# A recurrent layer's scans and roots in another order, an output product begun early, and the small products of the first projection moved

## The chip, the cores and the metric

The kernel runs on one core of a Trainium2 chip. It is one launch that computes the whole reference. The metric is the device time of the launch in microseconds (us), median over runs. The kernel is written engine by engine: each engine (TensorE, VectorE, ScalarE, GpSimd and the queue of SyncE) has a list of instructions of its own, and they meet only through semaphores. The order of each engine's list is the order of the code.

## The reference

Everything is float32. 512 tokens of 1024 channels go through two blocks:

```python
def first_block(...):            # one layer
    mod = silu(c) @ w_ada + b_ada                  # 6 vectors of 1024
    h = rmsnorm(x) * (1 + scale1) + shift1
    y = mixer(h)   # h @ w_in, causal convolution, gated delta rule and windowed attention, @ w_out
    x = x + gate1 * y
    h = rmsnorm(x) * (1 + scale2) + shift2
    x = x + gate2 * moe(h)       # 32 experts, top 4
def second_block(...):           # two layers; the modulation of each: silu(c_2) @ ada_w_2 + ada_b_2
    # layer 0: windowed attention, then mlp;  layer 1: recurrent_block, then mlp
def recurrent_block(h):
    z = h @ w_in;  xr, gate = split(z, 2)          # 1536 channels each
    xr = conv4(xr)                                  # centred depthwise convolution over 4 tokens
    for each direction (forward, reverse):
        r = sigmoid(xr @ w_a + b_a);  i = sigmoid(xr @ w_x + b_x)    # 16 blocks of 96 channels
        log_a = -8 * r * softplus(-lam);  a = exp(log_a)
        u = sqrt(-expm1(2 * log_a)) * (i * xr)
        h_t = a_t * h_(t-1) + u_t                   # scan over the tokens
    return ((h_forward + h_reverse) * gelu(gate)) @ w_out
```

In the mixer the decays need two small groups of columns of the first projection, `h @ w_in[:, 2048:2056]` (four channels a, four channels b).

## The kernel before

**The projection of the mixer** (`proj_pe`, `proj_act`, `proj_dve`). TensorE makes four column groups of 512: i = 0 to 2 are q, k and v (channels on partitions, convolved by VectorE), i = 3 is the gate z (tokens on partitions, four tiles t of 128 tokens), i = 4 the attention's queries, i = 5 its keys and values. The eight columns a and b are made in between, in two steps: line 518 makes four partial sums in one bank, ScalarE copies them to `abpart` (line 615, behind its twelve SiLUs of the convolutions), and four small products (line 544) with the selector `absel` add and turn them. These stand in the middle of the first tile of i = 3: at (i, t, k) = (3, 0, 4). `abw`, `absel` and `abpart` lie in rows 0 and 1 of `mixed`, which the SiLU of z overwrites tile by tile (line 621). VectorE then makes a, b ready (lines 578 to 583).

**The side sums.** At the same time VectorE multiplies 40 half slices of the modulation matrices (1 MB each) by the vector silu(c) and adds them up (`side_dve`, lines 376 and 378; called "half sums" here). They come through one slot of two halves: SyncE loads a half again when VectorE has read it (lines 165 and 333). After each eight of them TensorE sums over the partitions (`side_pe`, lines 397 and 385), ScalarE copies the result (`ada_act`, line 417) and sends it to DRAM with four DMAs (line 422). Sums 3 and 4 come last. VectorE's order is: half sums up to the 27th, then a wait for the sums of squares of TensorE (lines 586 and 588, released by line 526), the 28th, the decays' steps (lines 591 to 597), and the last twelve. All four compute engines then meet (`meet`, line 192), and the delta rule begins (line 712).

**The recurrent layer** (`rnn_pe`, `rnn_act`, `rnn_dve`, `rnn_pool`). Its input projection runs in eight steps of three channel tiles, in the order x0 x1 x2 z0 x3 z1 z2 z3 (line 2757). The gates run in eight units k = 2b + d (b a group of three channel tiles, d the direction): `gates(k, m)` is line 2771. In step i TensorE's order is gates(k, 0), gates(k, 1), block(i, 0), gates(k, 2), block(i, 1), for step 4 also all gates of unit 4, and block(i, 2). The gates have two pairs of banks, so gates(k, m) waits until ScalarE has read the gates two before (`gate_read`).

For each unit ScalarE does `front(k)`: two sigmoids for each tile (lines 2827, 2828), three tanh (2834), three exp (2838); and later `roots(k)`: one sqrt over three tiles (2842). Between different functions it loads a table. GpSimd squares the decays (2881). VectorE does `gate_in(k)` (2922, waits for all sigmoids), `one_minus(k)` (2928, waits for the squares; the sqrt waits for it), `scans(k)` (2935 waits for the sqrt, 2939 or 2941 are three scans, 2944 adds the two directions), and the convolutions `conv(n)` (2909 to 2917), each of which frees its bank for the next block of TensorE. `gelus` (2850) and `gated` (2951) make the last factor.

**The output product** (`rnn3_pe`, line 3001). Two halves h of 512 columns, for each of four token tiles t, sum over twelve channel tiles n. The weights lie in four slots, `RO_SLOT[h][n // 6]`: 2 and 4 for h = 0, 3 and 5 for h = 1. The order for t = 0 is slot 2, 4, 3, 5. It starts when all twelve tiles are gated. `rnn_out_sp` loads slot 2 early, slot 3 after unit 6, and slots 4 and 5 after the last scan; behind them stand the weights of the next layer. GpSimd's two loads of the layer norm start when all is gated. With t = 0, h = 0 finished, VectorE begins the residual (line 2044).

The order of the work around the change is written out by hand in `rnn_act` and `rnn_dve`; no planner is involved.

## Time and profile before

| | us |
|---|---|
| median of 3 runs | 3044.62 (3043.0 to 3049.29) |
| the profiled execution, its own time | 3045.79 |
| its span in the trace | 3044.1 |
| TensorE busy (matmuls) | 2788.8, 92% of the span |
| VectorE busy | 1134.7, 37% |
| ScalarE busy | 465.7, 15% |
| GpSimd busy | 235.7, 8% |

The projection of the mixer lies at 59 to 232 us of the span, the experts fill the middle, and the recurrent layer lies at 2290 to 2620 us. Positions in the text are us from the start of the span. "Granted clock" is TensorE's clock in a stretch as a share of full speed; 1.00 is 2.4 GHz and 0.50 is 1.2 GHz. Each matmul of float32 shows as two MATMUL instructions, so 8 products are "x16".

### The profile page before, as it was taken

Reading aid. Unit: us, or ns where it says so; the run is one execution under the profiler, and the core shown is the slowest. Engines: PE = TensorE matmul, PEld = TensorE weight load, DVE = VectorE, ACT = ScalarE, POOL = GpSimd, SP = SyncE. Lnnn points to the kernel's source line nnn. Section 1 sums busy time; section 2 is a strip of 40 time slices with the busy share of each in tenths; the row PEclk is TensorE's granted clock in tenths of the full one; section 3 lists DMA queues with packets and bytes.
Section 4 is the critical chain, followed back from the end, with each engine's and each line's share of the span. In section 5 each row is a group of like instructions: output and inputs, shape, how many; then the busy total and the mean of one; then the engine's idle time right before and its main releaser. Section 6 shows DMA issues by size and latency. Waiting matters only on the chain.

```text
span 3044.1 us, 37477 instructions
## 1 busy us (share of the span) xinstructions
PE 2788.8 (92%) x15695; PEld 1377.0 (45%) x15695; DVE 1134.7 (37%) x1419; ACT 465.7 (15%) x916; POOL 235.7 (8%) x364
## 2 busy tenths in 40 slices
PE   7898989698999999998996999999999988999998
PEld 3355765232323333333332465467654333546763
DVE  3855453411111111211114153455436552344544
ACT  1112042010000000000001143000023552200001
POOL 1000011111110011011011500000000100000000
PEclk9998989799999999999997999999999999999999
DMA  9765411889999999999998122122123223221310
GB/s 332 281 244 218 184 29 47 327 326 399 394 389 402 395 403 406 398 406 397 412 396 335 9 103 70 48 91 99 66 60 75 51 62 110 104 81 58 110 56 28
DMA packets 211795, 639.50 MB, mean 210 GB/s; under 512 B 75908, under 2 KB 77532, under 8 KB 170898
## 3 DMA queue, kind: packets, MB, share of 16 engines
q1 hardware_dynamic: 197778, 607.76, 52.9%
q0 software_dynamic: 13792, 29.39, 3.4%
q8 instruction: 120, 1.97, 0.3%
q14 instruction: 41, 0.33, 0.0%
q10 hardware_dynamic: 64, 0.07, 0.0%
HBM read 626.44 MB, written 15.23 MB: 211 GB/s over the span
## 4 chain that ended last, share of the span: by engine, by line
PE 51%; issue 33%; DVE 4%; DMA 4%; POOL 3%; POOLq 2%; ACT 2%; DVEq 1%; SPq 0%; ACTq 0%
PE ps L2421 10%; PE ps L2456 10%; PE ps L2757 4%; PE ps L2492 4%; PE ps L2136 3%; PE ps L3001 3%; PE ps L2388 2%; PE ps L2407 2%; PE ps L2303 2%; DMA slots<-in_ada_w_dram 2%; PE ps L1213 2%; POOLq L1656 2%; DMA slots<-in_w_ada_dram 2%; POOL work L1665 1%; PE ps L2771 1%
## 5 line engine op out<-in xcount | busy, mean ns | idle before, releaser
L1767 PE MATMUL ps<-slots,hT 128*32 128x512 f32 x5120 | 579.1, 598 | 17.5 <-DMA slots<-in_w_up_dram 6.7
L1767 PEld LDWEIGHTS ps<-slots,hT 128*32 128x32 f32 x5120 | 159.0, 110 | 412.8 <-issue 399.4
L2456 PE MATMUL ps<-slots,work 128*128 128x512 f32 x672 | 290.0, 593 | 5.3 <-DVE work L2532 2.8
L1803 PE MATMUL ps<-slots,work 128*32 128x512 f32 x2112 | 254.5, 609 | 26.6 <-DMA slots<-in_w_down_dram 19.3
L1918 DVE TENSOR_SCALAR stage<-ps 128x512 f32<-128x512 f32 (+1 forms) x47 | 32.2, 686 | 580.9 <-PE ps L1769 580.5
L2456 PEld LDWEIGHTS ps<-slots,work 128*128 128x128 f32 x672 | 127.2, 190 | 166.4 <-issue 162.0
L2421 PE MATMUL ps<-hT,slots 128*128 128x256 f32 x768 | 169.2, 380 | 4.7 <-issue 4.7
L1803 PEld LDWEIGHTS ps<-slots,work 128*32 128x32 f32 x2112 | 89.8, 111 | 157.2 <-issue 125.0
L2421 PEld LDWEIGHTS ps<-hT,slots 128*128 128x128 f32 x768 | 145.4, 190 | 29.1 <-issue 9.5
L2757 PE MATMUL ps<-hT,slots 128*128 128x512 f32 x352 | 156.8, 601 | 0.5
L2629 DVE TENSOR_TENSOR work<-work,ps 128x1024 f32<-128x1024 f32 x60 | 71.6, 1218 | 168.8 <-PE ps L2456 168.5
L1896 ACT ACTIVATE modA<-stage 128x512 f32<-128x512 f32 (+1 forms) x47 | 29.6, 630 | 635.9 <-DVE stage L1918 635.9
L2492 PE MATMUL ps<-slots,work 128*128 128x512 f32 x256 | 114.3, 608 | 5.3 <-DVE work L2594 5.3
L1938 DVE COPY modB<-ps 128x512 f32<-128x512 f32 x33 | 22.8, 691 | 229.6 <-PE ps L1806 221.9
L2757 PEld LDWEIGHTS ps<-hT,slots 128*128 128x128 f32 x352 | 66.3, 192 | 92.5 <-issue 92.5
L2588 DVE TENSOR_TENSOR work<-work,ps 128x1024 f32<-128x1024 f32 x42 | 50.7, 1220 | 129.9 <-PE ps L2421 129.2
L3001 PE MATMUL ps<-slots,work 128*128 128x512 f32 x192 | 84.8, 602 | 8.5 <-DVE work L2951 8.5
L2136 PE MATMUL ps<-slots,hT 128*128 128x512 f32 x192 | 85.9, 606 | 3.0 <-ACT hT L1084 3.0
L509 PE MATMUL ps<-hT,slots 128*128 128x512 f32 x192 | 84.6, 602 | 1.3 <-DVE hT L316 1.0
L2421 PE MATMUL ps<-slots 128*128 128x256 f32 x384 | 84.8, 379 | 0.0
L2522 ACT ACTIVATE work<-ps 128x1024 f32<-128x1024 f32 x6 | 6.1, 1024 | 500.3 <-PE ps L2421 500.3
L2492 PEld LDWEIGHTS ps<-slots,work 128*128 128x128 f32 x256 | 49.4, 195 | 67.1 <-issue 61.1
(585 smaller groups left out, 3442.3 us busy)
## 6 DMA issues: line engine op xcount, KB each, us to landing
slots<-in_w_up_dram SPq DMA_DIRECT2D x128, 2048.0 KB, 19.1
slots<-in_w_down_dram SPq DMA_DIRECT2D x64, 2048.0 KB, 17.7
slots<-in_mlp_w_dram SPq DMA_DIRECT2D x32, 2048.0 KB, 12.2
slots<-in_ada_w_dram SPq DMA_DIRECT2D x40, 1024.0 KB, 5.0
slots<-in_w_ada_dram SPq DMA_DIRECT2D x16, 1024.0 KB, 5.5
slots<-in_w_in_dram SPq DMA_DIRECT2D x5, 2048.0 KB, 14.7
slots<-in_rnn_w_in_dram SPq DMA_DIRECT2D x24, 384.0 KB, 4.2
slots<-in_w_ada_dram SPq DMA_DIRECT2D x4, 2048.0 KB, 18.8
```

The source lines that it names most:

```text
L509: ins = pe.matmul(ps[:, m], slots[:, s, k, m * P:(m + 1) * P], hT[:, k, :], start=k == 0, stop=k == KT - 1)
L1213: ins = pe.matmul(ps[:, 2 * (t % 2) + h], hT[:, k, t * P:(t + 1) * P], slots[:, 4 + h, k], start=k == 0, stop=k == KT - 1)
L1656: g.drain()
L1767: ins = pe.matmul(to, x[:, k, unit * UNIT:(unit + 1) * UNIT], upw[s][:, k % 2, col:col + CH], start=k == 0, stop=False)
L1803: ins = pe.matmul(to, actT[:, 4 * q + j, 64 * u + 32 * h:64 * u + 32 * h + 32], downw[sl[h]][:, j, half * CH:(half + 1) * CH], start=k == ...
L2136: ins = pe.matmul(ps[:, s], hT[:, k, t * P:(t + 1) * P], slots[:, s, k], start=k == 0, stop=k == KT - 1)
L2421: ins = pe.matmul(o, w[:, k, m * P:(m + 1) * P], x[:, k], start=k == 0, stop=k == HK - 1)
L2456: ins = pe.matmul(ps[:, bank + t], x[:, k, t * P:(t + 1) * P], w[:, k], start=k == 0, stop=k == HK - 1)
L2492: ins = pe.matmul(ps[:, 4 + 2 * (t % 2) + h], h1T[:, k, t * P:(t + 1) * P], slots[:, 2 + h, k], start=k == 0, stop=k == KT - 1)
L2629: ins = v.tensor_tensor(at, at, p_, ALU.add)
L2757: ins = pe.matmul(ps[:, m], slots[:, i % 3, k, m * P:(m + 1) * P], hT[:, k, :], start=k == 0, stop=k == KT - 1)
L3001: ins = pe.matmul(ps[:, 2 * (t % 2) + h], xr[:, n, t * P:(t + 1) * P], slots[:, RO_SLOT[h][n // 6], n % 6], start=n == 0, stop=n == RT - 1)
```

## The change

Four edits in the code:

1. Projection: the four small products move from (3, 0, 4) to (3, 2, 4), sixteen products and a side sum later; `abw`, `absel`, `abpart` move to rows 2 and 3 of `mixed`, which are overwritten later.
2. Projection, ScalarE: `ada_act(a, 3)` (copy and DMAs of sum 3) goes ahead of the wait for `gcol_out`, and the four DMAs of sum 4 (`ada_store`) go behind the meeting.
3. Recurrent layer: ScalarE's `roots(3)` goes from ahead of `front(4)` to the middle of it, behind its tanh. On VectorE `one_minus(3)` goes ahead of `conv(10)`, and `gate_in(4)`, `scans(3)`, `one_minus(4)` ahead of `conv(11)`.
4. Output product: for t = 0 the first six channel tiles of both halves run ahead of the wait for the last gated tiles. The order of the slots becomes 2, 3, 4, 5.

```diff
-        def ada_act(a, g):
+        def ada_act(a, g, store=True):
...
             a.drain()
+            if store:
+                ada_store(a, g)
+
+        def ada_store(a, g):
             j = 0
...
-        abw = mixed[:, 0, 0:KT * 32].rearrange("p (k c) -> p k c", k=KT)
-        absel = mixed[:, 0, KT * 32:KT * 32 + 2 * DH]
-        abpart = mixed[:, 1, 0:CH]
+        abw = mixed[:, 2, 0:KT * 32].rearrange("p (k c) -> p k c", k=KT)
+        absel = mixed[:, 2, KT * 32:KT * 32 + 2 * DH]
+        abpart = mixed[:, 3, 0:CH]
...
-                        if (i, t, k) == (3, 0, 4):
+                        if (i, t, k) == (3, 2, 4):
...
+            ada_act(a, 3)
             a.wait_ge(S("dn_scalar_dve"), DN_STEP["gcol_out"])
             a.activation(ek, ps[:, 4, 64:96], ACT.Exp).then_inc(S("dn_scalar_act"), 1)
-            ada_act(a, 3)
-            ada_act(a, 4)
+            ada_act(a, 4, store=False)
...
-            def front(k):
+            def front(k, between=None):
...
                     a.activation(M_[:, m], A_[:, m], ACT.Tanh, scale=lamn[:, d, n:n + 1])
+                if between is not None:
+                    roots(between)
                 a.drain()
...
             front(3)
-            roots(3)
-            front(4)
+            front(4, between=3)
             roots(4)
...
             conv(9)
             gate_in(3)
+            one_minus(3)
             conv(10)
-            one_minus(3)
+            gate_in(4)
+            scans(3)
+            one_minus(4)
             conv(11)
-            scans(3)
-            gate_in(4)
-            one_minus(4)
             scans(4)
...
         def rnn3_pe(pe):
-            pe.wait_ge(S("gated"), RT)
+            def first_halves():
+                pe.wait_ge(S("gated"), 6)
+                pe.wait_ge(S("z_read"), TT + RT - 1)
+                for h in range(2):
+                    take(pe, RO_SLOT[h][0], 4)
+                    for n in range(6):
+                        pe.matmul(ps[:, h], xr[:, n, 0:P], slots[:, RO_SLOT[h][0], n], start=n == 0, stop=False)
+                pe.wait_ge(S("gated"), RT)
...
                 for h in range(2):
-                    for n in range(RT):
-                        if t == 0 and n % 6 == 0:
-                            take(pe, RO_SLOT[h][n // 6], 4)
+                    for n in range(6 if t == 0 else 0, RT):
+                        if t == 0 and n == 6:
+                            take(pe, RO_SLOT[h][1], 4)
...
+            first_halves()
             for t in range(TT):
                 product(t)
...
                 proj_act(a); end()
+                ada_store(a, 4)
                 dn_act(a); end()
```

How the instructions stand, at three places. TensorE at the start of group i = 3 of the projection, before (`L549` is a product of the group, `L544` the four small products, `L397` and `L385` a side sum):

```order
L549 MATMUL ps<-slots,hT 128x512 [waits bank_free,landed1]
L549 MATMUL ps<-slots,hT 128x512 x3
L544 MATMUL ps<-work 128x8 [waits product_ab]
L544 MATMUL ps<-work 128x8 x3
L549 MATMUL ps<-slots,hT 128x512 x4
L549 MATMUL ps<-slots,hT 128x512 [waits bank_free]
L549 MATMUL ps<-slots,hT 128x512 x7
```

and now (the same lines are `L553` and `L548`):

```order
L553 MATMUL ps<-slots,hT 128x512 [waits bank_free]
L553 MATMUL ps<-slots,hT 128x512 x7
L397 MATMUL ps<-work,ones 32x512 [waits side_free]
L397 MATMUL ps<-work,ones 32x512 x3
L385 MATMUL ps<-modB,modA 32x512 x2
L385 MATMUL ps<-modG,modA 32x512 x2
L553 MATMUL ps<-slots,hT 128x512 [waits bank_free]
L553 MATMUL ps<-slots,hT 128x512 x3
L548 MATMUL ps<-work 128x8 [waits product_ab]
L548 MATMUL ps<-work 128x8 x3
L553 MATMUL ps<-slots,hT 128x512 x4
```

Sixteen products and a side sum now stand ahead of the wait for `product_ab` that stood behind it before.

ScalarE from the exp of unit 3 to the tanh of unit 4, before (`L2827`, `L2828` sigmoids, `L2834` tanh, `L2838` exp, `L2842` sqrt):

```order
L2838 ACTIVATE slots<-slots,triangles 128x512 x3
L2842 ACT_TABLE_LOAD
L2842 ACTIVATE slots<-slots 128x1536 [waits one_m]
L2827 ACT_TABLE_LOAD [waits scan_done]
L2827 ACTIVATE slots<-ps,triangles 128x512 [waits gate_ps]
L2828 ACTIVATE slots<-ps,triangles 128x512
L2827 ACTIVATE slots<-ps,triangles 128x512 [waits scan_done,gate_ps]
L2828 ACTIVATE slots<-ps,triangles 128x512
L2827 ACTIVATE slots<-ps,triangles 128x512 [waits scan_done,gate_ps]
L2828 ACTIVATE slots<-ps,triangles 128x512
L2834 ACTIVATE slots<-slots,triangles 128x512 [waits scan_done]
L2834 ACTIVATE slots<-slots,triangles 128x512 x2
```

and now (sigmoids `L2831` and `L2832`, tanh `L2838`, exp `L2844`, sqrt `L2848`):

```order
L2844 ACTIVATE slots<-slots,triangles 128x512 x3
L2831 ACT_TABLE_LOAD [waits scan_done]
L2831 ACTIVATE slots<-ps,triangles 128x512 [waits gate_ps]
L2832 ACTIVATE slots<-ps,triangles 128x512
L2831 ACTIVATE slots<-ps,triangles 128x512 [waits scan_done,gate_ps]
L2832 ACTIVATE slots<-ps,triangles 128x512
L2831 ACTIVATE slots<-ps,triangles 128x512 [waits scan_done,gate_ps]
L2832 ACTIVATE slots<-ps,triangles 128x512
L2838 ACTIVATE slots<-slots,triangles 128x512 [waits scan_done]
L2838 ACTIVATE slots<-slots,triangles 128x512 x2
L2848 ACT_TABLE_LOAD
L2848 ACTIVATE slots<-slots 128x1536 [waits one_m]
```

The sqrt of unit 3, with its wait, stands behind the six sigmoids and the tanh of unit 4; the number of table loads is the same.

VectorE around the last convolution, before (`L2928` one_minus, `L2909` to `L2917` a convolution, `L2935` to `L2944` scans, `L2922` gate_in):

```order
L2928 SCALAR_TENSOR_TENSOR slots<-stage,slots 128x512 [waits log_a] x2
L2928 SCALAR_TENSOR_TENSOR slots<-tmp,slots 128x512 [waits log_a]
L2909 TENSOR_SCALAR work<-ps,triangles 128x512 [waits product]
L2911 SCALAR_TENSOR_TENSOR work<-ps,triangles,work 128x510
L2913 SCALAR_TENSOR_TENSOR work<-ps,triangles,work 128x511
L2915 SCALAR_TENSOR_TENSOR work<-ps,triangles,work 128x511
L2917 COPY work<-work 32x512
L2935 TENSOR_TENSOR slots<-slots 128x1536 [waits mult_ready]
L2941 SCALAR_TENSOR_TENSOR slots<-slots 128x512 x3
L2944 TENSOR_TENSOR work<-work,slots 128x1536
L2922 TENSOR_TENSOR slots<-slots,work 128x1536 [waits gate_read]
```

and now (each line number is 5 higher):

```order
L2927 TENSOR_TENSOR slots<-slots,work 128x1536 [waits gate_read]
L2940 TENSOR_TENSOR slots<-slots 128x1536 [waits mult_ready]
L2946 SCALAR_TENSOR_TENSOR slots<-slots 128x512 x3
L2949 TENSOR_TENSOR work<-work,slots 128x1536
L2933 SCALAR_TENSOR_TENSOR slots<-stage,slots 128x512 [waits log_a] x2
L2933 SCALAR_TENSOR_TENSOR slots<-tmp,slots 128x512 [waits log_a]
L2914 TENSOR_SCALAR work<-ps,triangles 128x512 [waits product]
L2916 SCALAR_TENSOR_TENSOR work<-ps,triangles,work 128x510
L2918 SCALAR_TENSOR_TENSOR work<-ps,triangles,work 128x511
L2920 SCALAR_TENSOR_TENSOR work<-ps,triangles,work 128x511
L2922 COPY work<-work 32x512
```

The last convolution went from ahead of `scans(3)` and `one_minus(4)` to behind both.

## Rows read from the trace of the kernel before

**Rows 1.** Waits of TensorE over the span: us in total, times, longest
```profile
PE ps L1803 <- DMA slots<-in_w_down_dram: 19.3, 7, 4.8
...
PE ps L2771 <- ACT slots L2828: 14.2, 2, 7.9
...
PE ps L544 <- ACT work L615: 10.1, 1, 10.1
...
PE ps L3001 <- DVE work L2951: 8.5, 1, 8.5
```
**Rows 2.** Timeline of TensorE in the projection: start, us, instructions, idle before
```profile
228.30 1.06 PE L397 MATMUL ps<-slots,ones 128*32 128x512 f32 x8 [1.72 <-DVE slots L378]
...
232.49 3.65 PE L712 MATMUL ps<-slots,ones 128*128 128x512 f32 x4 [2.14 <-ACTq L192]
```
**Rows 3.** Timeline of VectorE in the projection
```profile
168.82 2.35 DVE L378 SCALAR_TENSOR_TENSOR slots<-slots,cT 128x2048 f32<-128x2048 f32 x1 [0.61 <-DMA slots<-in_ada_w_dram]
179.77 0.17 DVE L586 TENSOR_SCALAR small<-ps 128x16 f32<-128x16 f32 x1 [8.60 <-PE ps L526]
...
180.36 2.35 DVE L378 SCALAR_TENSOR_TENSOR slots<-slots,cT 128x2048 f32<-128x2048 f32 x1
```
**Rows 4.** Timeline of SyncE's queue in the projection
```profile
168.24 0.33 SPq L333 DMA_DIRECT2D slots<-in_ada_w_dram  x1
```
**Rows 5.** Chain that ended last, in the projection: start, us, what
```profile
190.63 5.65 DMA slots<-in_ada_w_dram
...
231.07 0.20 ACTq L422
...
232.19 0.26 ACTq L192
```
**Rows 6.** Window: us, busy and count of five engines, granted clock, DMA share, GB/s
```profile
228.00:230.00 2.00, 1.70 (x16) 0.34 (x16) 1.72 (x8) 0.68 (x2) 0.00 (x0) 1.00 0.00 1
```
**Rows 7.** Timeline of TensorE in the recurrent layer
```profile
2310.41 5.34 PE L2771 MATMUL ps<-work 96*32 96x512 f32 x32 [3.96 <-DVE work L2917]
...
2412.31 3.64 PE L2771 MATMUL ps<-work 96*32 96x512 f32 x32
2422.29 3.64 PE L2771 MATMUL ps<-work 96*32 96x512 f32 x16 [6.35 <-ACT slots L2828]
2425.86 7.90 PE L2757 MATMUL ps<-hT,slots 128*128 128x512 f32 x16
...
2452.62 3.64 PE L2771 MATMUL ps<-work 96*32 96x512 f32 x16 [7.90 <-ACT slots L2828]
...
2484.00 14.00 PE L2757 MATMUL ps<-hT,slots 128*128 128x512 f32 x32
...
2533.41 43.07 PE L3001 MATMUL ps<-slots,work 128*128 128x512 f32 x96 [8.45 <-DVE work L2951]
```
**Rows 8.** Timeline of ScalarE in the recurrent layer
```profile
2411.79 1.28 ACT L2842 ACT_TABLE_LOAD   x1
...
2448.51 1.48 ACT L2842 ACTIVATE slots<-slots 128x1536 f32<-128x1536 f32 x1 [14.62 <-DVEq L2929]
```
**Rows 9.** Timeline of VectorE in the recurrent layer
```profile
2384.94 2.96 DVE L2928 SCALAR_TENSOR_TENSOR slots<-stage,slots 128x512 f32<-128x512 f32 x2 [3.46 <-POOL stage L2881]
...
2439.46 3.46 DVE L2941 TENSOR_TENSOR_SCAN slots<-slots 128x512 f32<-128x512 f32 x3
2443.01 1.76 DVE L2944 TENSOR_TENSOR work<-work,slots 128x1536 f32<-128x1536 f32 x1
...
2446.56 1.29 DVE L2928 SCALAR_TENSOR_TENSOR slots<-stage,slots 128x512 f32<-128x512 f32 x2
...
2555.91 0.69 DVE L2044 TENSOR_TENSOR work<-ps,modG 128x512 f32<-128x512 f32 x1 [8.84 <-PE ps L3001]
```
**Rows 10.** DMA issues at 2531.2 to 2531.7, and at 2533.2 to 2533.7: us to landing
```profile
slots<-in_rnn_w_out_dram SPq DMA_DIRECT2D x1, 192.0 KB, 7.9
...
slots<-in_rnn_w_out_dram SPq DMA_DIRECT2D x1, 192.0 KB, 16.8
```

## What the change does to the time, worked out before it was run

> **What bounds the kernel now.** I first read the list of TensorE's waits over the span [rows 1]. TensorE is busy for 92% of the span, so what a change can win is one of its waits, and the change touches four of them: one of 10.1 us at the four small products (L544), two of 14.2 us together at the gates (L2771), one of 8.5 us at the output product (L3001). The reader is to see in the row that each was ended by ScalarE or VectorE, whose other share of busy time is small: it is order, not load, that makes them late. Then I read the timelines of TensorE, VectorE and ScalarE around each wait, to see what stands next in line, the chain of waits for the step from the projection to the delta rule, and last the windows for the granted clock and the landing times of the weights of the output product.
>
> The rest of the kernel (delta rule, experts, MLPs) begins at events of the parts ahead of it, not at a time of its own, so I let a gain in the projection pass through it whole; a rival below doubts that.
>
> **The projection.** TensorE's list: the wait for ScalarE's copy goes behind 16 more products and a side sum, some 16 us of work (14.0 and 2.0), longer than the wait of 10.1 us. So it goes, and all of TensorE's list behind it is at least 10.1 us earlier. But TensorE is not what ends this stage. VectorE's half sums are: the last one releases TensorE's fifth side sum at 228.30 [rows 2]. Their chain has one place where it waits for TensorE: 8.60 us ahead of L586, until 179.77 [rows 3]. With TensorE 10.1 us earlier this would be due at 169.7, ahead of the end of the 27th half sum (168.82 + 2.35 = 171.2), so the wait goes. Next is the load of the 28th half: issued at 168.24 [rows 4], and such loads take 5.65 us where the chain shows one in this stage [rows 5]; landed and seen by 173.7 or so. The 28th half sum started at 180.36 [rows 3] and would start at 173.6: 6.8 us earlier. From there a load follows a half sum and a half sum a load, so the shift stays until the end: TensorE is released at 221.5 in place of 228.30. Bounds: 8.6 us (the load is no limit) and 5 us (loads in a fuller queue).
>
> The meeting: ScalarE's four DMAs stood between its copy and the meeting, from 231.07 to the drain at 232.19 [rows 5], 1.1 us. Behind the meeting they lie beside TensorE's first sums of the delta rule (232.49, 3.65 us [rows 2]), for whose result ScalarE's next work waits; moved there they cost nothing. Sum 3's copy and DMAs go ahead of the wait for `gcol_out` (released by VectorE at 228); TensorE has made that sum by about 200, so they lie in idle time. If TensorE's sum 3 were late, the exp behind it would be late, and with it the meeting.
>
> The price: TensorE ends its own products at 226.6 (228.30 less 1.72) and now some 10 us earlier, about 216.5, and then idles 5 us until 221.5. In the old case, after 1.72 us, the granted clock was still 1.00 [rows 6]; after idles of 3.96, 6.35 and 7.90 us it had fallen: 32 instructions took 5.34 in place of 3.64, 16 took 3.64 in place of 1.82 [rows 7]. The side sum's 16 instructions, 2.0 us at 228 to 230, so take up to 4.0: 2.0 lost. L712 already ran slow after its 2.14 us [rows 2], so nothing more is lost there. Sum of this part: 6.8 + 1.1 - 2.0 = **5.9 us** earlier, between 3.0 (5 + 0 - 2.0) and 9.7 (8.6 + 1.1).
>
> **The recurrent layer.** Step 4 first. The gates' third tile of unit 4 waited 6.35 us for unit 4's first sigmoids, which stood behind sqrt(3). Now ScalarE goes on from its exp at 2411.79 [rows 8]: a table load (1.28) to 2413.1; gates (4,0) end at 2412.31 + 1.82 = 2414.1; two sigmoids of some 0.65 us to 2415.6. TensorE ends gates (4,1) at 2415.95. So it doesn't wait, keeps its clock (1.82 for the 3.64, and 7.0 for the 7.90 of the block behind [rows 7], 2.7 us in all), and begins step 5 at 2425.2 in place of 2434.0: 8.8 us earlier.
>
> Step 5. Its gates' third tile started at 2452.62, 4.1 us behind the start of sqrt(4) at 2448.51 [rows 7, 8]. Where does sqrt(4) stand now? ScalarE: sigmoids of unit 4's third tile to 2419.3, tanh (2.0) to 2421.2, table load and sqrt(3) to 2424.1 (one_minus(3) ends at about 2415, no wait). VectorE: scans(3) takes 7.1 us (1.76 for the product, 3.46, 1.76 and gaps [rows 9]), to 2431.3; one_minus(4), 2.0 us, to 2433.3. So sqrt(4) at 2433.4, 15.1 us earlier; the gates at 2437.5. TensorE comes there at 2425.2 + 3.6 + 7.1 = 2436.0 and idles 1.5 us, after which the clock was still full in rows 6, so the 2.6 us that the fallen clock cost there come back too: 17.7 us. The last convolution goes behind one_minus(4), to 2437.3; its bank is wanted at about 2446, so it costs nothing with 9 us of cover. From step 6 on the list of each engine is as before.
>
> Against this stands one thing. GpSimd's squares of unit 4 (three of 1.03 us) ran beside nothing that waits; now they fall between 2426 and 2430, beside scans(3) on VectorE. Where squares and one_minus ran side by side, one_minus's two instructions took 2.96 us in place of 1.29 [rows 9], 0.83 each. No row shows a scan beside a square. Bounds 0 and 3 x 0.83 = 2.5; I take the two of the row, 1.7. The idle then is 3.2 us, between 1.72 (clock kept) and 3.96 (fell, 1.7 us lost [rows 7]); bounds 0 and 2.7, and I take 0.8. Sum: 17.7 - 1.7 - 0.8 = **15.2 us**, between 12.5 and 17.7.
>
> The Trainium skill (SBUF — State Buffer, "SBUF: two separate sides") says that VectorE and GpSimd share a pair of ports as an exclusive lock, held for a whole instruction, when VectorE reads two SBUF inputs. The trace agrees for one_minus (2.96 for 1.29). By that rule scans, which read two inputs, would be held up by each square, and the part would give 17.7 - 2.5 - 0.8 = 14.4; without it, 17.7.
>
> **The output product.** Positions as in the old trace from here; all has moved alike. TensorE ends its last block at 2524.96 (2533.41 - 8.45 [rows 7]) and no longer waits: 12 products, 24 x 0.4375 us (14.00 / 32), to 2535.5. The last tile is gated by 2533.4. But next it wants slot 4, whose last DMA was issued at about 2531.2 and landed 7.9 us later, 2539.1 [rows 10]: an idle of 3.6. Six products, 5.3 us, to 2544.4; then slot 5, issued at 2533.2 and landed 16.8 us later, 2550.0: an idle of 5.6; six products, end at 2555.3. The old end of t = 0 was 2555.9 [rows 9]. So nearly the whole 8.45 us turns into waits for weights: 0.6 us gained. Nothing in the change loads them earlier: SyncE issues them behind the last scan. The clock falls in one idle of the two at least, 1.7 us as after 3.96. Sum 0.6 - 1.7 = -1.1; I take **-1.0**, between -2.7 and +0.6.
>
> The Trainium skill (TensorE: Matmul & The Clock Gate, "Why this matters for your kernels") says to leave no idle gaps between bursts of matmuls, since the clock then halves. Here the edit cuts one gap into two; by the rule both would cost, -2.7.
>
> **The sum.** 5.9 + 15.2 - 1.0 = 20.1 us. The profiled execution took 3045.79 (span 3044.1), so 3025.7 by it; it lies 1.2 above the median of 3044.62, and for the median I say **3024.5**.
>
> **The rivals.**
> (a) All doubtful prices are nothing: the squares don't hold up the scans, the clock holds in step 5 and at the output: 5.9 + 17.7 + 0.6 = 24.2, 3020; with the clock kept in the projection too, 3018.5. For it: an idle of 1.72 cost nothing. Against: the row of 2.96 us. 17%.
> (b) The projection's gain is lost: another chain of loads, or the delta rule that waits for something not shifted. 15.2 - 1.0 = 14.2, 3030.4. For it: the chain there is made of DMA pieces; against: each load is issued by a half sum. 17%.
> (c) The weights of slots 4 and 5 are no limit, and the 8.45 us go whole: 5.9 + 15.2 + 8.4 = 29.5, 3015. Against: the landing times. 6%.
> (d) The edits don't do what they say in step 5 (sqrt(4) as late as before, TensorE waits there as much longer as it came earlier) and the projection gives nothing: little but the 2.7 us of clock is left, 3042 to 3044. 5%.
> (e) Slower: the experts. Their weights come in one stream, and TensorE waits for it 19.3 us in 7 waits [rows 1]. The stage starts some 6 us earlier, and its waits depend on how stream and products lie against each other. If all 7 doubled and each also let the clock fall (7 x 1.7), it costs 19.3 + 11.9 = 31, and the time is 3044.6 - 20.1 + 31 = 3055.6. It decides from 20 us of new waits, 7 waits of 2.9 us. Against: stream and products start at the same event. 4%.
>
> **How the numbers follow.** The forecast's case, 3020 to 3029, has 51%. The range for 8 in 10 leaves out (c), (d), (e), and a little of the rest: 3016 to 3034. A measurement can tell 0.2%, 6.1 us. Faster by more: all but (d) and (e), 0.91; within: 0.05; slower: 0.04.
>
> **What would show it.** In the changed profile: no wait ahead of the four small products; none of VectorE for TensorE at the reciprocal (L586); the fifth side sum at about 221.5 and taking 4 us; the delta rule at about 226.6. In the recurrent layer no wait at the gates of unit 4 and one of 1.5 to 4 us at unit 5's, scans(3) longer than 7.1 if the squares hold it up; at the output product two waits for DMA of about 3.6 and 5.6 us in place of one for VectorE. I am wrong if the wait at L586 stays, if sqrt(4) is not some 15 us earlier against the start of step 4, or if the output product waits for no weights.

## The result, and the profile after

| | median us (all its executions) |
|---|---|
| before, measured beside it | 3046.95 (3043.0 to 3052.68, 4 executions) |
| changed | 3027.12 (3024.81 to 3029.81, 4 executions) |
| ratio | 0.9927, 95% interval 0.9913 to 0.9942 |

The change saves 19.8 us; 20.1 were predicted. Measured again beside another set of runs of the kernel before, the same kernel gave 3028.82 us and the ratio 0.9929 (0.9915 to 0.9943). The gain lies in the projection and in the recurrent layer, where it was placed, but step 5 of the layer gave less than the sum had. Two profiles of the same kernel also divide it differently.

The profiled execution took 3029.17 us. Its page, the length of the span and the busy time of each engine:

```profile
span 3027.5 us, 37477 instructions
...
PE 2792.3 (92%) x15695; PEld 1378.7 (46%) x15695; DVE 1139.2 (38%) x1419; ACT 465.6 (15%) x916; POOL 238.0 (8%) x364
```

The work is the same and the span 16.6 us shorter. The list of TensorE's waits over the whole span (us in total, times, longest):

```profile
PE ps L1807 <- DMA slots<-in_w_down_dram: 18.9, 7, 4.7
...
PE ps L1771 <- DMA slots<-in_w_up_dram: 8.5, 4, 3.6
...
PE ps L3013 <- DMA slots<-in_rnn_w_out_dram: 5.9, 2, 3.2
```

Of the waits of [rows 1], the one of 10.1 us at the small products is gone. So are the 14.2 us at the gates but for one piece of 3.67, and the 8.5 us for VectorE. In place of the last stand 5.9 us of waits for weights. The experts, which rival (e) feared for, wait 18.9 us where they waited 19.3; their waits at L1771 are 8.5 us where they were 6.7, and at a third line 4.6 where they were 6.6, so 32.0 us in all where it was 32.6.

**Projection.** TensorE's timeline (start, us, instructions, idle before and what ended it); L548 are the small products, L397 the side sums of the half sums, L716 the first product of the delta rule:

```profile
127.82 14.00 PE L553 MATMUL ps<-slots,hT 128*128 128x512 f32 x32
...
147.28 0.95 PE L548 MATMUL ps<-work 128*128 128x8 f32 x8
...
162.46 1.94 PE L397 MATMUL ps<-work,ones 128*32 128x512 f32 x8 [3.82 <-DVE work L378]
...
222.89 1.87 PE L397 MATMUL ps<-slots,ones 128*32 128x512 f32 x8 [2.62 <-DVE slots L378]
...
227.40 3.78 PE L716 MATMUL ps<-slots,ones 128*128 128x512 f32 x4 [0.79 <-ACTq L192]
```

No idle time stands ahead of L548. A new one of 3.82 us stands at 162.46, where an earlier side sum waits for VectorE's half sum. The fifth side sum starts at 222.89 in place of 228.30 [rows 2]. The wait for ScalarE's DMAs ahead of L716 has shrunk from 2.14 to 0.79 us, and the delta rule starts 5.1 us earlier. VectorE in the same stretch, and what replaced the wait of 8.60 us of [rows 3]:

```profile
170.71 2.35 DVE L378 SCALAR_TENSOR_TENSOR slots<-slots,cT 128x2048 f32<-128x2048 f32 x1 [0.46 <-DMA slots<-in_ada_w_dram]
173.41 0.17 DVE L590 TENSOR_SCALAR small<-ps 128x16 f32<-128x16 f32 x1 [0.35 <-PE ps L530]
...
175.24 2.35 DVE L378 SCALAR_TENSOR_TENSOR slots<-slots,cT 128x2048 f32<-128x2048 f32 x1 [1.33 <-DMA slots<-in_ada_w_dram]
```

The wait for TensorE is now 0.35 us, and the 28th half sum waits for its load instead. The chain of waits has the other half of the side sum, 8 instructions in 1.90 us, where the 8 ahead of it took 1.87; before, all 16 took 2.05 us (228.30 to 230.35):

```profile
222.89 1.87 PE ps L397 x8
224.76 1.90 PE ps L385 x8
```

**Recurrent layer.** TensorE from the third tile's gates of unit 4 on (L2775 gates, L2761 a block of the input product, L3001 and L3013 the output product):

```profile
2306.37 6.40 PE L2775 MATMUL ps<-work 96*32 96x512 f32 x32 [3.96 <-DVE work L2922]
...
2414.62 7.13 PE L2761 MATMUL ps<-hT,slots 128*128 128x512 f32 x16
2422.01 3.64 PE L2775 MATMUL ps<-work 96*32 96x512 f32 x32 [0.26 <-issue]
...
2436.39 3.64 PE L2775 MATMUL ps<-work 96*32 96x512 f32 x16 [3.67 <-ACT slots L2832]
2440.16 16.43 PE L2761 MATMUL ps<-hT,slots 128*128 128x512 f32 x32
2456.85 3.64 PE L2775 MATMUL ps<-work,slots 96*32 96x512 f32 x32 [0.26 <-issue]
...
2510.55 10.54 PE L3001 MATMUL ps<-slots,work 128*128 128x512 f32 x24 [0.26 <-issue]
...
2524.28 8.44 PE L3013 MATMUL ps<-slots,work 128*128 128x512 f32 x12 [3.19 <-DMA slots<-in_rnn_w_out_dram]
2535.42 25.16 PE L3013 MATMUL ps<-slots,work 128*128 128x512 f32 x58 [2.70 <-DMA slots<-in_rnn_w_out_dram]
```

The first of the two waits of [rows 7], 6.35 us, is gone and its block is back at 7.13 us (7.90). The second, 7.90 us, has become 3.67. Behind it 16 instructions of the gates take 3.64 us and 32 of the block 16.43, where [rows 7] have 14.00 for 32. ScalarE's sqrt of unit 4 and VectorE's work ahead of it:

```profile
2432.28 1.48 ACT L2848 ACTIVATE slots<-slots 128x1536 f32<-128x1536 f32 x1 [6.84 <-DVEq L2934]
```
```profile
2420.86 1.76 DVE L2940 TENSOR_TENSOR slots<-slots 128x1536 f32<-128x1536 f32 x1 [2.89 <-ACT slots L2848]
2422.70 5.05 DVE L2946 TENSOR_TENSOR_SCAN slots<-slots 128x512 f32<-128x512 f32 x3
2427.84 2.35 DVE L2949 TENSOR_TENSOR work<-work,slots 128x1536 f32<-128x1536 f32 x1
2430.32 1.29 DVE L2933 SCALAR_TENSOR_TENSOR slots<-stage,slots 128x512 f32<-128x512 f32 x2
```

The sqrt waits 6.84 us for VectorE's one_minus of unit 4. The three scans, which took 3.46 us in [rows 9], take 5.05, and the product behind them 2.35 in place of 1.76, while GpSimd squares (us of three squares, two in the first row):

```profile
2422.99 3.68 POOL L2886 TENSOR_TENSOR stage<-slots 128x512 f32<-128x512 f32 x2 [11.87 <-ACT slots L2844]
2426.63 1.95 POOL L2886 TENSOR_TENSOR tmp<-slots 128x512 f32<-128x512 f32 x1
```

**The ledger.** How much earlier the changed kernel reaches each place, from the two profiled executions (starts of the rows named). The last column is worked out in the same way from the profile of the second measurement of the changed kernel, an execution of 3033.78 us:

| place | before | changed | earlier by | gained in the piece | predicted | gained, second profile |
|---|---|---|---|---|---|---|
| first product of the delta rule | 232.49 | 227.40 | 5.1 | 5.1 | 5.9 | 6.6 |
| first gates of the recurrent layer | 2310.41 | 2306.37 | 4.0 | -1.1 | 0 | -7.4 |
| start of step 5's gates | 2434.02 | 2422.01 | 12.0 | 8.0 | 8.8 | 9.0 |
| start of step 6's gates | 2471.51 | 2456.85 | 14.7 | 2.7 | 6.4 | 5.3 |
| end of t = 0 of the output product (VectorE's second residual add) | 2556.68 | 2541.64 | 15.0 | 0.4 | -1.0 | -1.6 |
| span | 3044.1 | 3027.5 | 16.6 | 1.6 | 0 | 0.1 |

Step 4 gained 9.0 and not 8.0: the first gates took 6.40 us at the low clock in place of 5.34, 1.0 us that no edit touches. The 1.6 at the end is the same kind of thing: the last 128 instructions of the output product of the kernel's last stage took 56.90 us before, 55.20 here and 56.70 in the second profile. Both lie in code that the change left alone. So does the 7.4 us that the second profile lost between the delta rule and the recurrent layer; its span is 12.0 us shorter than that of before.

### The profile page after: what moved, and what is told of

The parts are those of the page before. It is cut to its first block, busy times and chain, and to the rows that moved or that the text cites. A ratio compares the mean times of both kernels' runs of the same rounds, so it can differ in the third digit from the quotient of the medians.

```text
span 3027.5 us, 37477 instructions
## 1 busy us (share of the span) xinstructions
PE 2792.3 (92%) x15695; PEld 1378.7 (46%) x15695; DVE 1139.2 (38%) x1419; ACT 465.6 (15%) x916; POOL 238.0 (8%) x364
## 4 chain that ended last, share of the span: by engine, by line
PE 50%; issue 33%; DMA 5%; DVE 4%; POOL 3%; POOLq 2%; ACT 2%; DVEq 1%; SPq 0%; ACTq 0%
PE ps L2425 10%; PE ps L2460 10%; PE ps L2761 4%; PE ps L2496 4%; PE ps L2140 3%; DMA slots<-in_ada_w_dram 2%; PE ps L3013 2%; PE ps L2392 2%; PE ps L2411 2%; PE ps L2307 2%; PE ps L1217 2%; POOLq L1660 2%; DMA slots<-in_w_ada_dram 2%; PE ps L2775 1%; POOL work L1669 1%
## 5 line engine op out<-in xcount | busy, mean ns | idle before, releaser
L1771 PE MATMUL ps<-slots,hT 128*32 128x512 f32 x5120 | 581.0, 600 | 19.2 <-DMA slots<-in_w_up_dram 8.5
L1771 PEld LDWEIGHTS ps<-slots,hT 128*32 128x32 f32 x5120 | 159.4, 110 | 415.7 <-issue 400.6
L2460 PE MATMUL ps<-slots,work 128*128 128x512 f32 x672 | 290.0, 593 | 5.3 <-DVE work L2536 2.8
L1807 PE MATMUL ps<-slots,work 128*32 128x512 f32 x2112 | 254.7, 609 | 26.1 <-DMA slots<-in_w_down_dram 18.9
L2761 PE MATMUL ps<-hT,slots 128*128 128x512 f32 x352 | 157.6, 604 | 0.5
L2496 PE MATMUL ps<-slots,work 128*128 128x512 f32 x256 | 112.6, 600 | 5.3 <-DVE work L2598 5.3
L2761 PEld LDWEIGHTS ps<-hT,slots 128*128 128x128 f32 x352 | 66.5, 193 | 92.4 <-issue 92.4
L3013 PE MATMUL ps<-slots,work 128*128 128x512 f32 x168 | 76.1, 613 | 5.9 <-DMA slots<-in_rnn_w_out_dram 5.9
## 6 DMA issues: line engine op xcount, KB each, us to landing
slots<-in_w_up_dram SPq DMA_DIRECT2D x128, 2048.0 KB, 18.9
slots<-in_w_down_dram SPq DMA_DIRECT2D x64, 2048.0 KB, 17.5
slots<-in_w_ada_dram SPq DMA_DIRECT2D x4, 2048.0 KB, 19.3
```

Source lines behind the costliest of these rows:

```text
L1771: ins = pe.matmul(to, x[:, k, unit * UNIT:(unit + 1) * UNIT], upw[s][:, k % 2, col:col + CH], start=k == 0, stop=False)
L1807: ins = pe.matmul(to, actT[:, 4 * q + j, 64 * u + 32 * h:64 * u + 32 * h + 32], downw[sl[h]][:, j, half * CH:(half + 1) * CH], start=k == ...
L2460: ins = pe.matmul(ps[:, bank + t], x[:, k, t * P:(t + 1) * P], w[:, k], start=k == 0, stop=k == HK - 1)
L2496: ins = pe.matmul(ps[:, 4 + 2 * (t % 2) + h], h1T[:, k, t * P:(t + 1) * P], slots[:, 2 + h, k], start=k == 0, stop=k == KT - 1)
L2761: ins = pe.matmul(ps[:, m], slots[:, i % 3, k, m * P:(m + 1) * P], hT[:, k, :], start=k == 0, stop=k == KT - 1)
L3013: ins = pe.matmul(ps[:, 2 * (t % 2) + h], xr[:, n, t * P:(t + 1) * P], slots[:, RO_SLOT[h][n // 6], n % 6], start=n == 0, stop=n == RT - 1)
```

## The experiments

Each has its own runs of the kernel before on the same chip, and its ratio is to these; "us faster" than before is worked out from the ratio, and with a second kernel beside it from the two medians. Besides the totals I read the start of one row in each profile, because the totals of single executions scatter: over the fourteen profiles that I have, the stretch from the delta rule to the recurrent layer, which no kernel changes, took between 2075 and 2090 us.

### Each edit by itself

**The projection's edits alone** (small products behind 16 more products, ScalarE's DMAs behind the meeting), the rest as before.

> The kernel before with the projection's edits alone (small products moved, sum 3's copy earlier, sum 4's DMAs behind the meeting). Theory P (the gain passes through whole): 5 us faster than before (the full change began the delta rule at 227.4 in place of 232.5), 4 to 6; the delta rule's L712 starts at 226 to 228. Rival Q (the experts and their stream of weights swallow it, since at the first gates of the recurrent layer only 4.0 of the 5.1 us were left): 1 us or less, with the delta rule early all the same.

Measured: 3040.11 us (3035.61 to 3047.21, 12 executions), ratio 0.9977 (0.9966 to 0.9989), 7.0 us faster. The delta rule starts at 225.86. Rival (b), that the whole gain of the projection is lost on the way, is out by this total, whose interval goes from 3.4 to 10.4 us. Whether a part of it is lost is open: the stretch from the delta rule to the recurrent layer took 2080.7 us on average in the eight profiles with both edits and 2077.4 in the five that keep the small products in their old place, with a scatter of several us within each group.

**The recurrent layer's order alone.**

> The kernel before with the recurrent layer's order alone (sqrt(3) inside front(4), scans(3) and one_minus(4) ahead of the last convolution). Theory P (the parts add): 11 to 13 us faster, no wait at the gates of unit 4, one of 3 to 4 us at those of unit 5, half clock behind it. Rival R (most of the 20 us of the whole change come from here, the projection gives nothing): 17 us or more.

Measured: 3033.33 us (3029.32 to 3037.58, 6), ratio 0.9953 (0.9939 to 0.9967), 14.3 us faster, a little more than expected. One wait of 3.67 us stands at unit 5's gates, as in the whole change; the gates behind it took 2.16 us and the block 15.32.

**The output product's start alone.**

> The kernel before with the output product begun with six channel tiles alone. Theory W (waits for the weights take the place of the wait for VectorE): between 1 us slower and 1 us faster, with two waits for DMA of about 3 us each in the output product. Rival V (the wait of 8.45 us goes for good): 6 to 8 us faster, no wait for DMA.

Measured: 3049.72 us (3044.43 to 3051.65, 11), ratio 1.0006 (0.9997 to 1.0016). TensorE at the output product:

```profile
2530.61 10.54 PE L2996 MATMUL ps<-slots,work 128*128 128x512 f32 x24 [0.26 <-issue]
...
2544.13 7.08 PE L3008 MATMUL ps<-slots,work 128*128 128x512 f32 x12 [2.98 <-DMA slots<-in_rnn_w_out_dram]
...
2554.48 15.70 PE L3008 MATMUL ps<-slots,work 128*128 128x512 f32 x32 [3.27 <-DMA slots<-in_rnn_w_out_dram]
```

The wait of 8.45 us for VectorE is gone and two waits for weights, 6.25 us together, stand in its place, with products between them that run slow (12 in 7.08 us in place of 5.25). From TensorE's first possible start to the end of t = 0 it is 31.8 us here (2562.4 less 2530.61) and 31.7 before (2556.68 less 2524.96). The edit by itself gains nothing, and rival (c) is out.

By their ratios the three parts alone add up to 7.0 + 14.3 - 1.8 = 19.5 us, and the whole gives 21.9 (0.9927 and 0.9929, mean); by the medians it is 17.5 and 20.1. Each interval reaches 3 to 4 us to either side, so they don't interact by more than can be measured.

**The two edits of the projection, one at a time.** The small products alone:

```diff
-                        if (i, t, k) == (3, 0, 4):
+                        if (i, t, k) == (3, 2, 4):
```

> The kernel before with the small products moved alone (edit 1). Theory P: the delta rule's first product starts 5 to 6 us earlier than before (at 227 to 228), its last wait being for ScalarE's four DMAs as before; 5 us faster. Rival (VectorE's half sums are a stream that its loads alone pace, and the wait at L586 was harmless): at 232, no gain.

Measured: 3047.04 us (3040.55 to 3056.44, 12), ratio 0.9998 (0.9983 to 1.0012). TensorE in its profile:

```profile
222.20 1.94 PE L397 MATMUL ps<-slots,ones 128*32 128x512 f32 x8 [6.20 <-DVE slots L378]
...
228.13 3.50 PE L712 MATMUL ps<-slots,ones 128*128 128x512 f32 x4 [2.14 <-ACTq L192]
```

The mechanism is there: the side sum is 6.1 us earlier, with 6.20 us of idle ahead of it; it runs at the low clock and loses 1.7 us, so the delta rule starts 4.4 us earlier. The total doesn't show it. In this profile 3.1 of the 4.4 us are gone at the first gates of the recurrent layer (2081.0 us from the delta rule, 2077.9 before). That is within the scatter of this stretch, and the interval of the total reaches to 5 us faster, so it may be noise; it stays open.

ScalarE's DMAs alone:

```diff
+            ada_act(a, 3)
             a.wait_ge(S("dn_scalar_dve"), DN_STEP["gcol_out"])
             a.activation(ek, ps[:, 4, 64:96], ACT.Exp).then_inc(S("dn_scalar_act"), 1)
-            ada_act(a, 3)
-            ada_act(a, 4)
+            ada_act(a, 4, store=False)
...
                 proj_act(a); end()
+                ada_store(a, 4)
```

> The kernel before with ScalarE's copy and DMAs moved alone (edit 2). Theory P: the DMAs of sum 4 leave the path, the wait ahead of L712 falls from 2.1 to 0.8 us and the delta rule starts 1.1 to 1.3 us earlier; the time within 1 to 2 us of before. Rival (ScalarE's next work is now late by as much): the start is earlier, but ScalarE's first exp of the delta rule comes no earlier.

Measured: 3047.53 us (3043.09 to 3057.83, 12), ratio 0.9999 (0.9987 to 1.0011), no change that can be told. The first product of the delta rule waits 0.79 us in place of 2.14 and starts at 231.83, 0.7 us earlier, though the side sum ahead of it started 0.7 us later here (228.99). ScalarE's first exp of the delta rule comes at 234.39 in place of 235.92, so the rival, that it comes no earlier, is out:

```profile
231.83 1.98 PE L716 MATMUL ps<-slots,ones 128*128 128x512 f32 x4 [0.79 <-ACTq L192]
```

Over all profiles the place is firm: with both edits the delta rule starts at 226.5 on average (225.57 to 227.82, eight profiles), with neither at 233.1 (232.47 to 234.42, four), 6.6 us apart.

**Half of the recurrent layer's edit**, ScalarE's order without VectorE's:

```diff
-            roots(3)
-            front(4)
+            front(4, between=3)
```

> The kernel before with ScalarE's part of the recurrent edit alone: sqrt(3) inside front(4), VectorE's order as before. Theory P: the wait ahead of unit 4's gates goes and step 4 ends 9 us earlier; the last convolution then ends at about 2426 in the old positions, scans(3) follow with unit 4's squares beside them (9.3 us in place of 7.1), then gate_in(4) and one_minus(4), so sqrt(4) comes at about 2440 in place of 2448.5: TensorE waits some 7 to 8 us at unit 5's gates, the gain is 8 to 9 us of the 12. Rival (VectorE's order is what counts, ScalarE's alone only moves the wait to unit 5's gates): under 3 us.

Measured: 3037.82 us (3031.95 to 3044.11, 11), ratio 0.9967 (0.9954 to 0.998), 10.1 us faster. TensorE:

```profile
2443.77 3.64 PE L2771 MATMUL ps<-work 96*32 96x512 f32 x16 [8.62 <-ACT slots L2828]
```

The wait at unit 4's gates is gone and the one at unit 5's is now 8.62 us, longer than before. So ScalarE's part takes away the first wait, and VectorE's order (the last convolution behind one_minus) cuts the second from 8.62 to 3.67. One point of what I expected was wrong. The scans beside the squares were to take longer here too, but they took their plain time, since with VectorE's old order the squares (2425.43 to 2428.46) fell beside the convolution. Of that only the last instruction was held up, a copy of 32x512 from `work` to `work`, 1.14 us in place of 0.42:

```profile
2430.60 3.46 DVE L2942 TENSOR_TENSOR_SCAN slots<-slots 128x512 f32<-128x512 f32 x3
```

**Without the output product's start**, the other edits in place.

> The changed kernel without its edit 4: the output product waits for all gated tiles as before. Theory W (edit 4 trades one wait of 8.5 us for two for the weights, with more slow clock): 1 to 3 us faster than the changed kernel, 22 to 23 us faster than before. Rival (edit 4 gains as it stands): 3 us or more slower than the changed kernel.

Measured: 3027.85 us (3024.03 to 3032.88, 6), ratio 0.9938 (0.9923 to 0.9952), against 0.9929 with it. The two can't be told apart; the expected gain of leaving it out is not shown, nor a loss.

### The two wrong terms

The prediction allowed 1.7 us for the squares and 0.8 for the clock. One theory (L) says that GpSimd's squares, running beside the scans, hold up one_minus(4) and sqrt(4), and that this alone makes the idle 3.67 us in place of 1.5. The other says that the order alone makes it. An experiment takes the squares of unit 4 away from GpSimd and gives them to ScalarE behind its exp:

```diff
+                if k == 4:
+                    a.drain()
+                    a.wait_ge(S("one_m"), 4)
+                    for m in range(BB):
+                        a.activation(squares[m], A_[:, m], ACT.Square).then_inc(S("log_a"), 1)
...
-                for m in range(BB):
+                for m in range(BB if k != 4 else 0):
```

> The changed kernel with the squares of unit 4 made by ScalarE behind its exp, in place of GpSimd. Theory L (VectorE's scans and GpSimd's squares shut each other out): scans(3) takes 7.1 us in place of 9.3, sqrt(4) comes 2.2 us earlier, the idle ahead of unit 5's gates falls from 3.7 to 1.5 and the clock stays full (block of 32 in 14.0 in place of 16.4, gates in 1.8 in place of 3.6): 6 us faster than the changed kernel, 4 at least. Rival (scans(3) is slow of its own place, beside ScalarE's exp and TensorE's reads): scans(3) stays at 9.3 and the time stays.

Measured: 3026.77 us (3016.76 to 3030.18, 6), ratio 0.9918 (0.9899 to 0.9936). The total can't be told from the changed kernel's: it is 2.1 us less by the medians, where 4 to 6 were expected. The stretch can be told. VectorE, and then TensorE:

```profile
2424.00 3.46 DVE L2951 TENSOR_TENSOR_SCAN slots<-slots 128x512 f32<-128x512 f32 x3
2427.55 1.76 DVE L2954 TENSOR_TENSOR work<-work,slots 128x1536 f32<-128x1536 f32 x1
```
```profile
2435.50 1.92 PE L2775 MATMUL ps<-work 96*32 96x512 f32 x16 [1.49 <-ACT slots L2832]
2437.56 13.99 PE L2761 MATMUL ps<-hT,slots 128*128 128x512 f32 x32
```

Without the squares beside them the scans are at 3.46 and the product at 1.76 again, the idle is 1.49 us, and the clock doesn't fall: 1.92 and 13.99 us. From the start of step 5 to that of step 6 it is 28.5 us, where the changed kernel took 34.8 in one profile and 32.2 in the other. The squares cost 2.2 us on VectorE (1.59 on the scans, 0.59 on the product).

The other term is the clock. In the changed kernel four products into a bank that nobody reads fill the idle time, and nothing else is changed:

```diff
                 block(i, 0)
+                if i == 5:
+                    for k in range(4):
+                        pe.matmul(ps[:, 3], slots[:, i % 3, k, 0:P], hT[:, k, :], start=k == 0, stop=k == 3)
                 gates(unit, 2)
```

> The changed kernel with four products more (8 instructions, 3.5 us, into a bank that nobody reads) ahead of the gates that wait in step 5. Theory C (the clock is what the idle costs beside its length): the gates still start when unit 5's first sigmoids are read, at the same distance from sqrt(4), but at full clock: gates 1.8 for 3.6 us, block of 32 14.0 for 16.4; 3 to 4.2 us faster than the changed kernel though it does more work. Rival (slow gates and block have another cause, as VectorE's or ScalarE's reads of PSUM): no gain.

Measured: 3030.11 us (3022.17 to 3033.34, 6), ratio 0.9933 (0.9917 to 0.9948), in the total the same as the changed kernel. TensorE:

```profile
2430.57 3.60 PE L2788 MATMUL ps<-hT,slots 128*128 128x512 f32 x8
2434.41 1.92 PE L2775 MATMUL ps<-work 96*32 96x512 f32 x16 [0.24 <-ACT slots L2835]
2436.47 13.99 PE L2761 MATMUL ps<-hT,slots 128*128 128x512 f32 x32
```

The extra products end 0.24 us before the gates may start, so the gates are no earlier for it; but these and the block behind them are at 1.92 and 13.99. Against 3.64 and 16.43 this is 4.2 us, all of it clock, while the same idle of 3.67 us in the recurrent layer's order alone cost 2.16 - 1.92 + 15.32 - 13.99 = 1.6. The second profile of the changed kernel, which ran beside this one, also lost 1.6 (2.08 and 15.40). Over the five profiles with an idle of 3.64 to 3.68 us here, it is 20.46 us from the start of these gates to those of step 6 in two and 17.85 in three, and 16.32 with the idle filled or shortened: the price was 4.1 us or 1.5. The expected 3 to 4.2 us are not in the total; a gain of this size is smaller than the total's scatter.

### A better version

The output product waits because its first 12 products take 10.5 us and TensorE is released by the weights of the next slots only 13.7 and 24.9 us behind its start. The second token tile (t = 1) needs the same first weights, and its banks are free behind one more read. So its first halves can go there too:

```diff
+                pe.wait_ge(S("z_read"), TT + RT)
+                for h in range(2):
+                    for n in range(6):
+                        pe.matmul(ps[:, 2 + h], xr[:, n, P:2 * P], slots[:, RO_SLOT[h][0], n], start=n == 0, stop=False)
                 pe.wait_ge(S("gated"), RT)
...
-                    for n in range(6 if t == 0 else 0, RT):
+                    for n in range(6 if t < 2 else 0, RT):
```

> The changed kernel in which TensorE also runs the first six channel tiles of token tile t = 1, both halves, behind those of t = 0 and ahead of all that needs slots 4 and 5. Theory W (the wait for VectorE turned into waits for the weights): 10.5 us of work cover the two waits; no wait for DMA or one under 1 us, full clock through the product, 6 to 9 us faster than the changed kernel. Rival (the output stage is bound by something behind it, the layer norm's chain, or a new wait for the last gelu's bank): under 2 us, with a new wait.

Measured: 3016.2 us (3014.37 to 3024.84, 6), ratio 0.9899 (0.9882 to 0.9915), 31 us faster than before and 12.6 faster than the changed kernel beside it (9 by the two ratios). TensorE at the output product:

```profile
2503.55 10.54 PE L3001 MATMUL ps<-slots,work 128*128 128x512 f32 x24 [0.26 <-issue]
2513.93 10.46 PE L3005 MATMUL ps<-slots,work 128*128 128x512 f32 x24
2524.23 20.76 PE L3017 MATMUL ps<-slots,work 128*128 128x512 f32 x48
```

No wait for weights is left. From the start of the output product to the last residual add of t = 1 it is 42.2 us (2503.55 to 2545.79), and 51.7 in the changed kernel (2510.55 to 2562.24), or 53.7 in its second profile, which ran beside this one: 9.5 to 11.5 us from this edit. Each of the six times lies below each of the six of the changed kernel beside it.

Last, this and the squares on ScalarE together:

> The changed kernel with both variants that gained in their own stretch: ScalarE makes unit 4's squares, and the output product begins with two token tiles. If their gains add (6.3 us from the start of step 5 to step 6, and 11 to 13 us from the first gates to the end of token tile 1), 36 to 39 us faster than before, about 3010 us. Rival (the squares' gain is lost in the output stage, since both end at the same last scan and its weights): 30 to 33 us faster, as the two tiles alone, and a wait for DMA in the output product.

Measured: 3016.9 us (3010.66 to 3025.29, 6), ratio 0.9898 (0.9881 to 0.9915), the same as the two tiles alone, and not the expected further gain. Inside the recurrent layer the gain is there: from its first gates to the end of t = 1 239.1 us, against 242.8 with the two tiles alone and 255.9 and 254.2 in the two profiles of the changed kernel. Its profiled execution had the longest stretch ahead of the recurrent layer of all, 2089.9 us, so 3.7 us can't be read from the totals of six executions. The kernel to keep is that with two tiles; whether the squares add anything to it is open.

## Why the prediction was right, step by step

**What bounds.** Right: each of the four waits was one of order, and each reordering took it away or changed what ended it.

**TensorE's list 10.1 us earlier.** Wrong, though it cost nothing. The list was to be earlier by the whole wait; at the end of its own products it is at 220.27 (222.89 less 2.62) and was at 226.58, 6.3 us. At the row of 162.46 the list would have been 12.8 us earlier (171.45 before, against 158.64), the 10.1 and 3.2 of low clock that the old wait had cost, less 0.5 by which this execution was late at the start of the group. But that side sum now waits 3.82 us for VectorE, which the prediction hadn't looked at, and the low clock behind it takes 2.6 more: the side sum's first 8 instructions take 1.94 us in place of 1.06, its other 8 as much longer, and L530 behind it 6.98 in place of 6.10. It stayed without effect since VectorE, not TensorE, ends the stage.

**Half sums, 6.8 us.** Right, though not in the first profile. There the 28th half sum started at 175.24 in place of 180.36, 5.1 us earlier: its load was read rightly as the next limit, but the 27th half sum itself stood at 170.71 and not at 168.82 [rows 3], 1.9 us of scatter in the loads ahead. In the second profile the 27th stood at 169.00 and the 28th at 173.53, 6.8 us earlier. On average it started at 174.2 in the eight profiles with both edits and at 181.0 in the five that keep the small products in their old place. The sum itself had a slip: 168.24 + 5.65 is 173.9 and not 173.6. In the first profile the side sum was 5.4 us earlier, with the small products moved alone 6.1, in the second profile 7.0.

**DMAs behind the meeting, 1.1 us.** Right: the wait at L716 is 2.14 less 0.79, or 1.35 us, shorter. By itself it moved the start by 0.7.

**Clock in the projection, -2.0.** Right in size: TensorE idled 2.62 us and not 5, since its list was late as said above, but the 16 instructions took 3.7 us (222.89 to 226.6) in place of 2.05, so 1.7 was lost. 5.4 + 1.35 - 1.7 gives the 5.1 us of this profile; over all profiles it is 6.6, and 5.9 were predicted. The price isn't firm: behind idles of 4.30 and 4.34 us in two of the variants the first 8 instructions took 1.07 and 1.06 us.

**Step 4, 8.8 us.** Right: 9.0, in both profiles. Neither wait nor low clock is left there.

**Step 5, 6.4 us.** Here the order was right and the size was not: 2.7 us in this profile, 5.3 in the second one of the same kernel (32.2 us in place of 37.5). sqrt(4) started at 2432.28, 16.2 us earlier [rows 8]; 3.0 of these had been won ahead of step 4, so 13.2 are its own, where 15.1 less the 1.7 of the squares were predicted. Its order is as foreseen, and two terms were too small. The squares cost 2.2 and not 1.7, because the product behind the scans was held up as well as the scans; so the idle was 3.67 and not 3.2. And the clock, for which I took 0.8 between 0 and 2.7, cost 4.2 in one profile and 1.6 in the experiment with the same idle. The upper bound of 2.7 came from the gates and the block of step 4 in the old trace, where the wait had been longer, 6.35 us; so the price doesn't follow the length of the idle. With the terms as measured the working comes out: 17.7 - 8.8 = 8.9, less 2.2 and 4.1 is 2.6, less 2.2 and 1.5 is 5.2, against 2.7 and 5.3 in the two profiles.

The granted clock at the place, from windows of the changed kernel (columns as in [rows 6]; the granted clock is the third number from the end):

```profile
2432.00:2434.00 2.00, 0.71 (x2) 0.00 (x0) 1.77 (x3) 1.71 (x2) 0.00 (x0) 1.00 0.00 0
2434.00:2436.00 2.00, 0.00 (x0) 0.00 (x0) 1.78 (x3) 1.99 (x3) 0.00 (x0) 0.71 0.00 0
2436.00:2438.00 2.00, 1.61 (x8) 0.40 (x12) 1.90 (x2) 1.50 (x3) 0.00 (x0) 0.50 0.00 0
2442.00:2444.00 2.00, 2.00 (x4) 0.94 (x3) 1.40 (x1) 1.95 (x4) 0.00 (x0) 0.50 0.00 0
2444.00:2446.00 2.00, 2.00 (x4) 0.79 (x4) 0.00 (x0) 1.99 (x4) 0.47 (x1) 0.73 0.00 0
```

The clock fell from full to half, 2.4 to 1.2 GHz, in the idle time ahead of 2436.39 and was back only behind 2444. In the second profile it was still 1.00 through the same idle (2436 to 2440), 0.93 from 2440 to 2442, 0.50 from 2442 to 2444, and 1.00 again from 2446: there it fell only when the gates were nearly done, and fewer instructions ran slow.

**The rule on the shared ports.** The Trainium skill (SBUF — State Buffer, "SBUF: two separate sides") was weighed with 2.5 us for the squares in place of 1.7. The trace agrees that scans are held up, which no row had shown. The scan under way when the squares began took its plain time, and the two behind it 0.8 us more each:

```profile
2422.70 1.23 DVE L2946 TENSOR_TENSOR_SCAN slots<-slots 128x512 f32<-128x512 f32 x1
...
2423.84 2.00 DVE L2946 TENSOR_TENSOR_SCAN slots<-slots 128x512 f32<-128x512 f32 x1
...
2425.76 1.99 DVE L2946 TENSOR_TENSOR_SCAN slots<-slots 128x512 f32<-128x512 f32 x1
```

The third square held up the product behind the scans by 0.6. So each of the three squares cost something, as by the rule, and together they cost 2.2 us, between the 1.7 taken and the 2.5 of the bound.

**Output product, -1.0.** Right in its mechanism, and in size between two profiles. The landings were as read from [rows 10]: TensorE was released 13.7 and 24.9 us behind the start of the product, and the sum had 14.1 and 25.0. In the first profile the waits were 3.19 and 2.70 us where 3.6 and 5.6 stood in the sum, since the products between them ran at the low clock, 8.44 us in place of 5.25. In the second profile these ran at the full clock:

```profile
2525.40 5.39 PE L3013 MATMUL ps<-slots,work 128*128 128x512 f32 x12 [3.20 <-DMA slots<-in_rnn_w_out_dram]
2536.42 28.14 PE L3013 MATMUL ps<-slots,work 128*128 128x512 f32 x60 [5.64 <-DMA slots<-in_rnn_w_out_dram]
```

The product started at 2511.66 there, so the releases came 13.7 and 24.8 us behind it, as in the first, and the second wait was 5.64 us. So the low clock between the waits cost nothing in the first profile: it lay in time that was waited away. Behind the second wait it does cost: the granted clock was 1.00 there in the first profile and 0.50 from 2536 to 2540 in the second. From the start of the product to the end of t = 0 it took 31.1 us in the first, 33.1 in the second and 31.7 before, a gain of 0.6 and a loss of 1.4. By the rule of the Trainium skill (TensorE: Matmul & The Clock Gate, "Why this matters for your kernels") both gaps were to cost. The clock did fall in or behind one of them in each profile, but only behind the second gap did it set the time; behind the first the release by a DMA did. The working has two slips of rounding: 0.6 less two prices of 1.7 is -2.8 and not -2.7, and in step 4 the terms 6.35 and 2.7 make 9.1 and not 8.8.

**The rivals.** (a) is out by its reason, as each of the doubtful prices was paid in at least one profile. (b) is out as it stands, by the projection alone; that a part of its gain is lost is not excluded. (c), (d) and (e) are out by the output product alone, the rows above and the experts' waits, 32.0 us where they were 32.6. That the total came within half a microsecond of the predicted gain is in part luck: step 5 gave 3.7 us less in this profile, the output product 1.6 more, and the two ledgers' own totals are 16.6 and 12.0 where the medians are 19.8 and 20.4 apart.

## What to carry to other kernels

- When a wait is taken away, write down what releases the next instruction and when; where that is a DMA issued at an unchanged place, the gain is nothing until there is work to lay in front of it. Twelve more products that needed only what was there turned a part worth nothing into one worth 9.5 to 11.5 us.
- A short idle of TensorE has a second price in the slow instructions behind it, and it isn't fixed. Take it from several rows, and as nothing where a DMA sets the next release.
- Judge an edit worth 1 to 4 us by the distance between two rows inside its stretch, not by the total, if the rest of the kernel scatters by more.

## What the runs showed of the hardware

- A tensor_tensor_scan on VectorE is held up by a GpSimd elementwise instruction beside it: three scans of 128x512 took 5.05 us in place of 3.46 (1.23 for the one already under way, 2.00 and 1.99 for the others), a 128x1536 product 2.35 in place of 1.76, and GpSimd's squares themselves 1.84 to 1.95 each in place of 1.03.
- After the same idle of 3.67 us, 48 instructions took 20.07 us in one execution (3.64 + 16.43) and 17.48 in another (2.16 + 15.32); at the full clock, with the idle filled, 15.91. After an idle of 1.49 us they took 15.91 too. Of five profiles with this idle two had the higher price and three the lower.
- ScalarE squares three tiles right behind an exp in 0.58 us each, with no table load between.
- The landings of the output product's weights released TensorE 13.7 and 24.9 us behind the start of the product in one profile of the changed kernel and 13.7 and 24.8 in the other. In three other kernels with this edit it was 13.4 to 13.6 and 23.9 to 24.8.
- With these releases fixed, twelve instructions between them took 8.44 us at the low clock or 5.39 at the full one, and the wait behind them was 2.70 or 5.64 us: the low clock was paid out of the wait.
